# adaLN as dot products on VectorE over transposed weights, with its weight tiles dealt out anew

## The chip, the cores and the metric

The kernel runs on one core of a Trainium2 chip. The core has five engines with instruction streams of their own, which wait for each other by semaphores: TensorE (PE; its weight loads are PEld), VectorE (DVE), ScalarE (ACT), GpSimd (POOL) and SyncE (SP), here the issuer of most DMAs. The metric is the device time of one execution in microseconds.

## What is computed

Two transformer blocks over 256 tokens of 1024 channels in fp32, batch 1. The first block has two layers, each an adaLN, a hybrid mixer (gated linear attention and SSD), and a dense SwiGLU FFN (layer 0) or eight SwiGLU experts, top 2 (layer 1). The second block has one layer: adaLN, Hyena and neighbourhood attention, and PEER, which gathers rows of a table of 16384 experts. What the change touches is adaLN alone: three projections of a silu'd condition vector to 6 x 1024 values each, the third for two conditions.

```python
s = jax.nn.silu(c)
mod = s @ ada_w[l] + ada_b[l]                              # (1, 1024) @ (1024, 6144), l = 0, 1
sh1, sc1, g1, sh2, sc2, g2 = split(mod, 6)
h = rmsnorm(x, norm1_w[l]) * (1.0 + sc1) + sh1
x = x + g1 * hybrid_mixer(h, ...)
h = rmsnorm(x, norm2_w[l]) * (1.0 + sc2) + sh2
x = x + g2 * (swiglu(h, ...) if l == 0 else moe_swiglu(h, ...))
...
m = jax.nn.silu(cond) @ p['w_ada'] + p['b_ada']            # second block, for c and for c_ctx
```

## The kernel before

Activations lie transposed, channels on partitions (`xT`, `hT`: 128 x 8 x 256). Weights stream through `Ring`, five slots of 128 x 4096 fp32 (2 MB each). `place` hands the slots out in a fixed round, and SP, in `sp`, waits ahead of each load until the last user of that slot is done; so the loads are in a strict order, and one that waits holds all behind it. The experts' weights go through the same memory in halves (`parts`), and in PEER some of it holds gathered rows.

Each of the three adaLN matrices is 12 tiles of 512 output columns (class `Ada`, line 251), 2 MB each, 36 in all. The modulation has to end up with channels on partitions (`mods`), eight columns for each of the six vectors. For a tile and one condition, `ada_rows` (line 1192) on VectorE multiplies the eight 128 x 512 blocks of the tile by the eight columns of the condition and sums them into `accb`: one start (line 1199) and seven operations (line 1202). Then `ada_columns` (line 563) on TensorE sums `accb` over the partitions by four products with a column of ones, and `ada_add` (line 1206) on VectorE adds the bias and writes `mods`. `accb` is single: the rows of a tile wait until TensorE has read those of the one before (`acc_readers`). The tiles `ada2[0:4]` have two conditions and do all of it twice.

Four tiles (`ada0[0:4]`: shift and scale of the first norm) are done at the start. The others are dealt out by the list `behind` (line 262): six in mixer 0, twenty in the dense FFN, six in mixer 1 (`ada2[0:6]`, four of them with two conditions). They are worked off by `background()`, which stands at matching places of the streams of TensorE and VectorE; each call finishes the tile before and starts the next. In the mixers it stands behind the projections of z, qk, v and xs on TensorE and three times behind g, ahead of the state products (line 661); on VectorE behind `la`, behind the copies of q and k (lines 1250 and 1252), twice behind the copies of v (line 1274), and three times behind the scan `cum`, ahead of the states and the copy `dc` (line 1318). Lines 1256 to 1272 are the softplus, the scan and the exponentials of the gated linear attention, line 1284 its masked copies. In the FFN (line 747; lines 536 and 765 are the products) it stands three times in each of the seven steps; a step is gate and up (four pairs of 128 columns) and then the down product of the step before. SP loads in a step gate, up, two adaLN tiles, the down tile of the step before, and one more adaLN tile.

The second block's stage has no adaLN work. Its attention loop runs over 16 turns (8 heads x 2 halves of tokens): `peak(i + 2)` and `scaled(i + 1)` on VectorE, and between them TensorE's scores and transposes and ScalarE's copies and exponentials. TensorE works off eight pieces of gate projections (`fill`) beside q, k, kc and the first five turns. The bias of the attention holds one ring slot to the end of the loop.

PEER's dot products (line 1765) are `tensor_tensor_reduce` of 128 x 1024 from a gathered row tile and a token tile in PSUM, with a sum to one column; the trace calls them `CUSTOM_DVE_ANT_0`.

## Time and profile before

| | us |
|---|---|
| median of 3 runs | 3107.36 (3101.91 to 3108.8) |
| the profiled execution | 3108.38 |
| its span | 3106.6 |
| TensorE busy | 2660.6 (86%) |
| VectorE busy | 2012.0 (65%) |
| ScalarE busy | 1121.1 (36%) |

A row of a timeline gives start, duration, engine, line of the kernel, operation, output <- inputs and how many such instructions it merges; the brackets give the time that the engine was idle ahead of it, and what released it. Matmuls of fp32 appear as two instructions each. "ring" is a weight slot, "arena" the shared scratch, "ps" PSUM. Stages on the span: start to 47 us, mixer 0 to 255, dense FFN 272 to 619, mixer 1 642 to 872, experts 921 to 1925, second block to 2400, PEER to the end.

### The profile page before, as it was taken

The page shows a single profiled execution, that of the slowest core. Times are in us where ns is not written, and L with a number is a line of the kernel's source. Part 1 is how long each engine was busy: PE and PEld are TensorE (multiplying, and loading weights), DVE is VectorE, ACT ScalarE, POOL GpSimd, SP SyncE. Part 2 cuts the span into 40 slices and gives each one's busy share as a digit, 9 for nine tenths or more (in the row PEclk, how much of TensorE's full clock was granted, in tenths as well). Part 3 has the DMA queues.
Part 4 walks back from the last instruction along what each step waited for, and adds up shares of the span by engine and source line. Part 5 has one row for each costly group of instructions (what it writes and reads, how often), then busy time and mean ns, then how long its engine had stood idle before and what let it go on. Part 6 is the DMA issues. An engine that isn't in the chain of part 4 may idle for free. (4 is left out here: it accounts for less than half of the span.)

```text
span 3106.6 us, 34837 instructions
## 1 busy us (share of the span) xinstructions
PE 2660.6 (86%) x13674; PEld 2258.2 (73%) x13674; DVE 2012.0 (65%) x2882; ACT 1121.1 (36%) x1243; POOL 256.3 (8%) x280
## 2 busy tenths in 40 slices
PE   5866999986569999999999998699778898888787
PEld 4645788855457888888888886565666788887777
DVE  4553443346538889899998996353632777777764
ACT  1211000011127777777777775210340222222221
POOL 0000000000000000000000000000000233433341
PEclk8968999987669999999999999899898999988898
DMA  7702665635029999999999994521014799999996
GB/s 295 273 25 92 260 277 213 285 133 216 1 74 353 338 359 359 356 341 357 357 358 341 356 359 159 208 82 54 28 55 149 305 380 418 418 418 419 418 418 285
DMA packets 102139, 822.66 MB, mean 265 GB/s; under 512 B 11144, under 2 KB 13320, under 8 KB 13712
## 3 DMA queue, kind: packets, MB, share of 16 engines
q1 hardware_dynamic: 64816, 550.99, 46.3%
q0 software_dynamic: 36864, 268.45, 21.1%
q8 instruction: 111, 1.82, 0.2%
q10 hardware_dynamic: 288, 0.91, 0.1%
q14 instruction: 60, 0.49, 0.0%
HBM read 819.26 MB, written 1.05 MB: 264 GB/s over the span
## 5 line engine op out<-in xcount | busy, mean ns | idle before, releaser
L1491 DVE TENSOR_TENSOR ring_r<-ring,arena_r 128x2048 fp32r<-128x2048 f32 x336 | 770.2, 2292 | 12.2 <-ACT arena_r L1784 0.8
L1784 ACT ACTIVATE arena_r<-ring 128x2048 fp32r<-128x2048 f32 x336 | 645.0, 1920 | 10.7
L536 PE MATMUL ps<-h,ring 128*128 128x256 f32 (+1 forms) x2112 | 486.2, 393 | 48.8 <-ACT h L1784 31.8
L536 PEld LDWEIGHTS ps<-h,ring 128*128 128x128 f32 (+1 forms) x2112 | 408.0, 194 | 123.3 <-issue 53.6
L820 PE MATMUL ps<-arena_r 128*128 128x512 f32 x896 | 354.2, 395 | 1.5 <-DVE arena_r L1496 1.5
L822 PE MATMUL ps<-arena_r 128*128 128x512 f32 x896 | 349.7, 390 | 0.0
L821 PE MATMUL ps<-ring_r,arena_r 128*128 128x512 f32 x896 | 349.1, 390 | 0.0
L1784 ACT ACTIVATE arena<-ps 128x512 f32<-128x512 f32 (+2 forms) x204 | 103.2, 506 | 625.9 <-PE ps L536 415.7
L1144 PE MATMUL ps<-sel,arena 128*128 128x128 f32 x1904 | 254.4, 300 | 72.8 <-ACT sel L1784 72.8
L1144 PEld LDWEIGHTS ps<-sel,arena 128*128 128x128 f32 x1904 | 247.7, 215 | 79.4 <-ACT sel L1784 79.3
L1144 PE MATMUL ps<-sel,ring 128*128 128x128 f32 x2192 | 268.6, 285 | 41.1 <-ACT sel L1784 41.0
L1144 PEld LDWEIGHTS ps<-sel,ring 128*128 128x128 f32 x2192 | 262.2, 201 | 46.2 <-ACT sel L1784 46.0
L1202 DVE SCALAR_TENSOR_TENSOR accb<-ring,small,accb 128x512 f32<-128x512 f32 x280 | 210.5, 752 | 9.9
L1784 ACT ACTIVATE arena<-arena 128x4 f32<-128x4 f32 (+10 forms) x188 | 83.7, 445 | 360.2 <-DVE arena L1765 202.4
L1765 DVE CUSTOM_DVE_ANT_0 accb<-ring,ps 128x1024 f32<-128x1024 f32 x137 | 167.3, 1221 | 66.1 <-DMA ring<-in_uv,arena 63.1
L820 PEld LDWEIGHTS ps<-arena_r 128*128 128x128 f32 x896 | 168.3, 188 | 35.5 <-DVE arena_r L1496 1.8
L822 PEld LDWEIGHTS ps<-arena_r 128*128 128x128 f32 x896 | 168.3, 188 | 35.6
L821 PEld LDWEIGHTS ps<-ring_r,arena_r 128*128 128x128 f32 x896 | 168.5, 188 | 34.2
L1784 ACT ACT_TABLE_LOAD x62 | 79.5, 1283 | 301.6 <-DVE arena L1765 69.7
L1765 DVE CUSTOM_DVE_ANT_0 accb<-arena,ps 128x1024 f32<-128x1024 f32 x119 | 145.3, 1221 | 65.6 <-DMA arena<-in_uv,arena 63.3
L820 PE MATMUL ps<-arena_r,h_r 128*128 128x512 f32 x448 | 179.2, 400 | 6.6 <-DVE ring_r L1491 6.6
L822 PE MATMUL ps<-arena_r,h_r 128*128 128x512 f32 x448 | 175.9, 393 | 0.0
(237 smaller groups left out, 3037.6 us busy)
## 6 DMA issues: line engine op xcount, KB each, us to landing
ring<-in_moe_w_gate SPq DMA_DIRECT2D x112, 1024.0 KB, 5.8
ring<-in_moe_w_up SPq DMA_DIRECT2D x112, 1024.0 KB, 6.1
ring<-in_moe_w_down SPq DMA_DIRECT2D x112, 1024.0 KB, 5.6
ring<-in_ada_w SPq DMA_DIRECT2D x24, 2048.0 KB, 12.5
ring<-in_w_ada SPq DMA_DIRECT2D x12, 2048.0 KB, 10.4
ring<-in_w_in SPq DMA_DIRECT2D x10, 2048.0 KB, 11.3
ring<-in_ffn_w_gate SPq DMA_DIRECT2D x7, 2048.0 KB, 12.0
ring<-in_ffn_w_up SPq DMA_DIRECT2D x7, 2048.0 KB, 16.5
```

The lines of the kernel that those rows point to most:

```text
L536: last = e.matmul(out, a, b, start=(i == 0), stop=(i == len(pairs) - 1))
L820: e.matmul(out, xs[0], ws[0], start=start, stop=False, skip_group_check=True)
L821: e.matmul(out, xs[0], ws[1], start=False, stop=False, skip_group_check=True)
L822: return e.matmul(out, xs[1], ws[0], start=False, stop=stop, skip_group_check=True)
L1144: last = e.matmul(ps.banks[2 * t + c // 4][:, 128 * (c % 4):128 * (c % 4) + 128], rows[:, 1024 + 128 * c:1152 + 128 * c], m.diag[g % 2][:, ...
L1202: v(e.scalar_tensor_tensor(a, tile[:, k, :], t.s[:, i:i + 1], a, ALU.mult, ALU.add), ("rows", t.name))
L1491: v(e.tensor_tensor(m.low[parts.slot[unit]], parts.buf[unit], m.high[unit_at[unit] % NHIGH].bitcast(F32), ALU.subtract), ("low", unit))
L1765: v(e.tensor_tensor_reduce(m.waste, row_buffer(i)[0][:, 0:1024], x, 1.0, 0.0, ALU.mult, ALU.add, m.dots[:, i:i + 1]), ("dots", g))
L1784: A.mark(e.activation(out, src, func, **kw), name)
```

## The change

- The adaLN matrices are transposed on the host (`turned`): a tile of 2 MB holds 4 x 128 output channels on partitions, each with its 1024 weights in a row. The condition comes from the host repeated over the partitions (`cond`, 128 x 1024 each) and is silu'd on ScalarE there.
- A tile and condition is four `tensor_tensor_reduce` on VectorE (generator `ada`), each with the bias as the start value and one column of `mods` as the result. `ada_columns`, `ada_add` and `acc_readers` go. The product's elementwise output is dumped in `waste`.
- `some(pieces, n)` does n of these pieces at the places where `background()` stood on VectorE: 8, 4, 6 and 6 in a mixer; in the FFN 2 behind each activation, 3 in steps 2 to 5; 2 in each turn of the attention loop.
- The tiles are dealt out anew: four at the start and six in mixer 0 as before; fourteen in the FFN, two in each step, among them the four with two conditions; four in mixer 1 (16 pieces); eight in the attention loop.
- Loads: the FFN's step has five loads instead of six. In the second block the eight tiles are loaded behind `w_in`'s last tiles through the four slots other than that of the bias.
- The condition of the first block is loaded on ScalarE's queue between `pv` and `cs`; those of the second are loaded ahead of the norm behind mixer 0, and one of them again, into `accb`, ahead of the norm behind mixer 1.

```diff
-            def __init__(self, name, w, n, s, stride, ncond, bias, outs):
-                self.name, self.w, self.n, self.s, self.stride = (name, n), w[n], n, s, stride
-                self.ncond, self.bias, self.outs = ncond, bias, outs
-                self.at = n % 2 if name == "ada0" and n < 4 else 0
-        ada0 = [Ada("ada0", T["ada_w0"], n, small[:, 0:8], 1, 1, "ada_b0", [mod[0]]) for n in range(12)]
-        ada1 = [Ada("ada1", T["ada_w1"], n, small[:, 0:8], 1, 1, "ada_b1", [mod[1]]) for n in range(12)]
-        ada2 = [Ada("ada2", T["w_ada"], n, small[:, 8:24], 2, 2 if n < 4 else 1, "b_ada", [m2[:, 0, :], m2[:, 1, :]])
-                for n in range(12)]
-        behind = {"mix0": ada0[4:10], "ffn0": ada0[10:12] + ada1 + ada2[6:12], "mix1": ada2[0:6]}
+            def __init__(self, name, w, n, s, ready, bias, outs, waste):
+                self.name, self.w, self.n, self.s, self.ready = (name, n), w[n], n, s, ready
+                self.bias, self.outs, self.waste = bias, outs, waste
+        waste = arena[:, ARENA - 1024:ARENA]
+        cond0, cond1, cond2 = accb, arena[:, 2560:3584], arena[:, 3584:4608]
+        ada0 = [Ada("ada0", T["ada_w0"], n, [cond0], "silu c", "ada_b0", [mod[0]], waste) for n in range(12)]
+        ada1 = [Ada("ada1", T["ada_w1"], n, [cond0], "silu c", "ada_b1", [mod[1]], waste) for n in range(12)]
+        ada2 = [Ada("ada2", T["w_ada"], n, [cond1, cond2], "silu c2", "b_ada", [m2[:, 0, :], m2[:, 1, :]], waste)
+                for n in range(4)]
+        ada2 += [Ada("ada2", T["w_ada"], n, [accb], "silu c2 again", "b_ada", [m2[:, 0, :]], selb)
+                 for n in range(4, 12)]
+        behind = {"mix0": ada0[4:10], "ffn0": ada0[10:12] + ada1[0:2], "mix1": ada1[8:12], "second": ada2[4:12]}
+        for n in range(4):
+            behind["ffn0"] += [ada1[2 + n], ada2[n]]
+        behind["ffn0"] += ada1[6:8]
...
                         load(("up", f), T["ffn_w_up"][f])
-                        load_ada(hidden.pop(0))
-                        load_ada(hidden.pop(0))
+                        load_ada(hidden[2 * f])
+                        load_ada(hidden[2 * f + 1])
                         if f:
                             load(("down", f - 1), T["ffn_w_down"][f - 1])
-                        if hidden:
-                            load_ada(hidden.pop(0))
                     load(("down", 6), T["ffn_w_down"][6])
...
             load("bias", T["bias"])
+            kept = ring.slot["bias"]
+            ring.order, ring.n = [(kept + 1 + i) % NSLOT for i in range(NSLOT - 1)], 0
+            hidden = list(behind["second"])
             for n in range(8, 10):
                 load(("w_in2", 512 * n), T["w_in2"][n])
+                load_ada(hidden.pop(0))
+            for t in hidden:
+                load_ada(t)
             for name in ("w_hy", "w_na"):
                 for n in range(2):
                     load((name, n), T[name][n])
+            at = ring.n % (NSLOT - 1)
+            ring.order, ring.n = ring.order[at:] + ring.order[:at] + [kept], 0
             for n in range(2):
...
-            def ada_columns(t, among=range(8)):
-                b = bank(t.name, among)
-                e.wait_ge(*V["rows", t.name])
-                for c in range(t.ncond):
-                    for m in range(4):
-                        at = 512 * (t.at + c) + 128 * m
-                        last = e.matmul(b[:, 4 * c + m:4 * c + m + 1], accb[:, at:at + 128], ones[:, 0:1],
-                                        start=True, stop=True)
-                P.mark(last, t.name)
...
                 done(("w_in", l, "xs"))
-                background()
...
                 done(("w_in", l, "g"))
-                for _ in range(3):
-                    background()
...
-            def ada_rows(t):
-                tile = cols_of(t.name)
+            def ada(t):
+                tile = v4(ring.buf[t.name], 4)
                 e.wait_ge(*ring.loaded[t.name])
-                if acc_readers:
-                    e.wait_ge(*P[acc_readers.pop()])
-                for c in range(t.ncond):
-                    a = accb[:, 512 * (t.at + c):512 * (t.at + c) + 512]
-                    v(e.tensor_scalar(a, tile[:, 0, :], t.s[:, c:c + 1], None, ALU.mult))
-                    for k in range(1, 8):
-                        i = t.stride * k + c
-                        v(e.scalar_tensor_tensor(a, tile[:, k, :], t.s[:, i:i + 1], a, ALU.mult, ALU.add),
-                          ("rows", t.name))
-                ring.emptied[t.name] = V.now
-            def ada_add(t):
-                b = taken(t.name)
-                for c in range(t.ncond):
-                    v(e.tensor_tensor(t.outs[c][:, 4 * t.n:4 * t.n + 4], b[:, 4 * c:4 * c + 4],
-                                      pvc(t.bias, 4 * t.n, 4), ALU.add))
-                emptied(t.name)
+                e.wait_ge(*A[t.ready])
+                for m in range(4):
+                    o = 4 * t.n + m
+                    for s, out in zip(t.s, t.outs):
+                        v(e.tensor_tensor_reduce(t.waste, tile[:, m, :], s, 1.0, pvc(t.bias, o), ALU.mult, ALU.add,
+                                                 out[:, o:o + 1]))
+                        ring.emptied[t.name] = V.now
+                        yield
+            def some(pieces, n):
+                for _ in range(n):
+                    next(pieces, None)
             V.stage("ada")
             e.wait_ge(*in_pv)
-            e.wait_ge(*A["silu c"])
-            ada_rows(ada0[0])
+            some(ada(ada0[0]), 4)
             rstd(("norm1", 0), taken(("norm1", 0))[:, 0:256], 1.0 / D, scr_end[:, 2048:2304])
-            ada_rows(ada0[1])
-            for n in range(2):
-                ada_add(ada0[n])
-                ada_rows(ada0[n + 2])
-            for n in range(2, 4):
-                ada_add(ada0[n])
-            acc_readers.append(ada0[3].name)
+            for t in ada0[1:4]:
+                some(ada(t), 4)
...
-                background()
+                some(hidden, 8)
                 v(e.tensor_scalar(m.qT, v4(taken(("qk", l, 0)), 2), 0.125, None, ALU.mult))
                 emptied(("qk", l, 0))
                 v(e.tensor_copy(m.kT, v4(taken(("qk", l, 1)), 2)))
                 emptied(("qk", l, 1))
-                background()
+                some(hidden, 4)
...
-                for _ in range(2):
-                    background()
+                some(hidden, 6)
...
-                for _ in range(3):
-                    background()
+                some(hidden, 6)
...
-                        if j == 1:
-                            background()
-                    background()
-                    background()
+                        some(hidden, 3 if 2 <= f < 6 else 2)
...
+            hidden = chain.from_iterable(ada(t) for t in behind["second"])
             for i in range(16):
                 if i + 2 < 16:
                     peak(i + 2)
                 if i + 1 < 16:
                     scaled(i + 1)
+                some(hidden, 2)
             ring.emptied["bias"] = V.now
...
+            e.dma_start(cond0, T["cond"][0]).then_inc(in_c[0], 16)
             e.dma_start(cs, T["cs"]).then_inc(in_cs[0], 16)
             A.stage("ada")
             e.wait_ge(*in_pv)
-            a(small[:, 0:8], pvc("c", 0, 8), ACT.Silu, "silu c")
-            a(small[:, 8:24], pvc("c2", 0, 16), ACT.Silu, "silu c2")
+            e.wait_ge(*in_c)
+            a(cond0, cond0, ACT.Silu, "silu c")
...
+                e.wait_ge(*in_c2)
+                for cond in (cond1, cond2):
+                    a(cond, cond, ACT.Silu, "silu c2")
...
+                e.wait_ge(*in_c2_again)
+                a(accb, accb, ACT.Silu, "silu c2 again")
...
+                if l == 0:
+                    for cond, src in ((cond1, T["cond"][1]), (cond2, T["cond"][2])):
+                        e.dma_start(cond, src).then_inc(in_c2[0], 16)
+                else:
+                    e.dma_start(accb, T["cond"][1]).then_inc(in_c2_again[0], 16)
                 norm(("norm2", l), xT, mod[l][:, 24:32], hT, scr_end, ("hT", "norm2", l))
...
+    def turned(w):
+        return w.T.reshape(-1, 4, 128, 1024).transpose(0, 2, 1, 3).reshape(-1, 128, 4096)
...
+        "cond": np.repeat(np.stack([x["c"][0], x["c_2"][0], x["c_ctx_2"]])[:, None, :], 128, axis=1),
```

## Rows read from the trace of the kernel before

**Rows 1.** Stages: start:end, length, PE, PEld, DVE, ACT, POOL busy, PEclk, DMA share, GB/s.

```profile
272.20:619.40 347.20, 323.55 (x1504) 284.74 (x1504) 130.01 (x208) 12.01 (x29) 0.00 (x0) 0.94 0.58 239
...
921.00:1925.00 1004.00, 997.50 (x4613) 830.30 (x4614) 894.80 (x554) 727.79 (x478) 0.00 (x0) 1.00 0.91 341
```

**Rows 2.** Groups by line on VectorE: shapes, count, busy us, mean ns, idle before.

```profile
L1202 DVE SCALAR_TENSOR_TENSOR accb<-ring,small,accb 128x512 f32<-128x512 f32 x280 | 210.5, 752 | 9.9
...
L1765 DVE CUSTOM_DVE_ANT_0 accb<-ring,ps 128x1024 f32<-128x1024 f32 x137 | 167.3, 1221 | 66.1 <-DMA ring<-in_uv,arena 63.1
```

**Rows 3.** Timeline of VectorE in PEER: start us, us, engine, line, operation.

```profile
2453.72 1.22 DVE L1765 CUSTOM_DVE_ANT_0 accb<-ring,ps 128x1024 f32<-128x1024 f32 x1
...
2454.99 1.22 DVE L1765 CUSTOM_DVE_ANT_0 accb<-ring,ps 128x1024 f32<-128x1024 f32 x1
```

**Rows 4.** Timeline of the start, all engines; in brackets idle time before and its releaser.

```profile
1.17 0.47 ACTq L1809 DMA_DIRECT2D cs<-in_cs  x1
...
13.28 5.59 PE L536 MATMUL ps<-arena,cs 128*128 128x256 f32 x16 [13.28 <-DMA cs<-in_cs]
...
19.24 0.42 DVE L1170 TENSOR_SCALAR arena<-ps 128x256 f32<-128x256 f32 x1
...
21.49 0.49 DVE L1199 TENSOR_SCALAR accb<-ring,small 128x512 f32<-128x512 f32 x1
...
41.98 0.16 DVE L1209 TENSOR_TENSOR mods<-ps,pv 128x4 f32<-128x4 f32 x1 [1.83 <-PE ps L570]
```

**Rows 5.** Timeline of VectorE in mixer 0.

```profile
92.23 0.69 DVE L1252 COPY arena<-ps 128x512 f32<-128x512 f32 x1 [6.21 <-PE ps L536]
...
99.25 0.43 DVE L1256 TENSOR_SCALAR arena<-arena 128x512 f32<-128x512 f32 x1
...
113.72 1.42 DVE L1274 COPY arena<-ps 128x512 f32<-128x512 f32 x2
...
128.87 2.67 DVE L1284 COPY_PREDICATED arena<-ms,ps 128x128 f32<-128x128 uint32 x8
...
139.77 0.49 DVE L1199 TENSOR_SCALAR accb<-ring,small 128x512 f32<-128x512 f32 x1
...
162.82 0.19 DVE L1318 COPY arena<-ps 128x32 f32<-128x32 f32 x1
```

**Rows 6.** Timeline of TensorE in mixer 0.

```profile
106.59 0.95 PE L570 MATMUL ps<-cs,accb 128*128 128x1 f32 x8
...
124.70 13.98 PE L536 MATMUL ps<-h,ring 128*128 128x256 f32 x64
...
155.90 5.08 PE L661 MATMUL ps<-arena 128*128 128x256 f32 x12
```

**Rows 7.** Timeline of VectorE in mixer 1.

```profile
686.35 0.69 DVE L1252 COPY arena<-ps 128x512 f32<-128x512 f32 x1 [6.21 <-PE ps L536]
...
700.49 0.43 DVE L1256 TENSOR_SCALAR arena<-arena 128x512 f32<-128x512 f32 x1
...
745.10 2.67 DVE L1284 COPY_PREDICATED arena<-ms,ps 128x128 f32<-128x128 uint32 x8
...
777.85 0.19 DVE L1318 COPY arena<-ps 128x32 f32<-128x32 f32 x1
```

**Rows 8.** Timeline of TensorE in the dense FFN.

```profile
272.22 29.98 PE L536 MATMUL ps<-h,ring 128*128 128x256 f32 x128 [8.68 <-ACT h L1784]
...
315.74 16.59 PE L536 MATMUL ps<-h,ring 128*128 128x256 f32 x64 [4.34 <-issue]
...
347.68 14.06 PE L765 MATMUL ps<-arena,ring 128*128 128x256 f32 x64
```

**Rows 9.** Loads into the ring, 290 to 380 us (dense FFN): issue to landing.

```profile
DMA to landing us min/median/max: 7.5/13.3/17.7
```

**Rows 10.** Timeline of VectorE in the attention loop.

```profile
2276.79 0.42 DVE L1653 SCALAR_TENSOR_TENSOR arena<-ps,ring 128x256 f32<-128x256 f32 x1 [7.03 <-ACT arena L1784]
...
2281.12 0.42 DVE L1653 SCALAR_TENSOR_TENSOR arena<-ps,ring 128x256 f32<-128x256 f32 x1 [1.99 <-ACT arena L1784]
```

60 lines of the change are left out of this document (8 added, 52 removed).

## The prediction, made before the change was run

> **What bounds the kernel now.** I read the view by stages first. In the experts' stage TensorE is busy 997.5 of 1004 us at a granted clock of 1.00 (2.4 GHz), so nothing that VectorE does is worth anything there, and the change leaves that stage alone. In the dense FFN it is busy 323.55 of 347.20 us: 24 us are open [rows 1]. The time lies where TensorE and VectorE wait for each other, so I read both engines' timelines through the two mixers, the FFN and the attention loop. In mixer 0 the projections of g end at 138.7, but the state products start only at 155.9 [rows 6]: between them stand the tiles of adaLN, one after the other, VectorE's rows, TensorE's columns, VectorE's addition. Their operands are ready; the queue order holds them back. In mixer 1, with two conditions in four of its six tiles, the same piece of code runs from 686.35 to 777.85, 91.5 us, against 70.6 us (92.23 to 162.82) in mixer 0 [rows 5, 7].
>
> **Price of a piece.** Before, a tile costs seven operations of 752 ns [rows 2] and a start, some 6 us, then columns and an addition. After, it is four dot products of 128x1024, each one `tensor_tensor_reduce`. The same operation stands in PEER: 1221 ns, and one starts 1.27 us after the other, 2453.72 to 2454.99 [rows 2, 3]. I take 1.27 us. That row reads one operand from PSUM, the new ones both from SBUF, so the price is not quite shown: a lower one has no row for it; the upper end is a rival, below. The rows operation at 752 ns for 512 columns has two SBUF operands and against 1221 ns for 1024 it shows no doubling [rows 2].
>
> The Trainium skill speaks against this ("Vector Engine (DVE) Microarchitecture Reference", "Points that are easy to get wrong"): a scalar_tensor_tensor with two non-bf16 SBUF sources halves throughput, as both read ports are taken and none is left for the accumulator's readback. By it a piece would be some 2.2 to 2.3 us by estimate, and the sum would be that of the second rival. The rows operation in this trace, two fp32 sources in SBUF without an accumulator, isn't slowed; with one, no row shows it.
>
> **The parts, by stage** (times on the axis of before).
> 1. Start. Old: the last addition ends at 41.98 + 0.16 [rows 4]. New: four tiles are 16 pieces, 20.3 us, and the 2.25 us of the norm's root (19.24 to 21.49 [rows 4]) in front of the last twelve. The condition, now 512 KB, goes on ScalarE's queue ahead of `cs`. `cs` was issued at 1.17 and held the first TensorE work until 13.28 [rows 4]: with `pv` some 890 KB in 12.5 us, 71 KB a us, so half a MB more delays the norm by up to 7.4 us, and at the 341 GB/s of the experts' stage [rows 1] by 1.5. VectorE's root starts then at 20.7 to 26.6 instead of 19.24 [rows 4], and 2.25 + 12 x 1.27 later it is done: 38.1 to 44.0. That is a gain of 4 to a loss of 2; I take the middle, a gain of 1.
> 2. Mixer 0. Copy of k done at 92.9, four pieces 5.1: the softplus starts at 98.0 instead of 99.25; its chain to the end of the copies of v, 15.9 us, ends at 113.9; six pieces: 121.5 [rows 5]. TensorE loses three column groups ahead of the end of g (0.95 us each [rows 6], counted at 0.8 since they overlap their neighbours), which comes at 136.3 instead of 138.7 [rows 6]. VectorE's masked copies to the scan took 10.9 us (128.87 to 139.77) [rows 5], 1.6 of it the addition and its wait (as the 1.83 at 41.98 [rows 4]): 9.3, so 130.8; six pieces: 138.4. From the start of the state products to the copy behind them are 6.9 us (155.90 to 162.82) [rows 5, 6]: 136.3 + 6.9 = 143.2; VectorE alone would be there at 143.0. Gain 162.8 - 143.2 = 19.6. What is late next is TensorE's own projections; the tiles are there, since their slots come free with z, qk and v as before.
> 3. FFN. By 7 steps: gate and up 28.1 us, down 14.06 [rows 8]. Before, six tiles a step went through five slots; now five, so each kind has its slot. Gate and up of the next step are issued together when the products of this one end, land within 13.3 us [rows 9], and the down products of 14.06 us [rows 8] cover that by 0.4 (without this cover it costs the difference in each of five steps). Step 1 has no down in front; its gate already has a free slot and only up must land, 7.5 [rows 9] + 0.4, taken as 8. Sum: 29.98 + 8 + (16.59 + 14.06) + 5 x 28.1 + 7 x 14.06 = 307.6, against 347.2 [rows 1, 8]: gain 39.6. VectorE has 12 pieces, 15 us, in steps of 42 us; two activations of the broadcast conditions and their loads lie beside the norm and the first products.
> 4. Mixer 1, by the same steps: copy of k done at 687.0 [rows 7], +5.1, +15.9, four last pieces +5.1: 713.1; masked copies and scan: 725. g ends 43.4 us behind the copy of k (136.3 - 92.9): 730.4; +6.9 = 737.3, instead of 777.85 [rows 7]. Gain 40.5. VectorE has 5 us of slack there.
> 5. ScalarE issues two loads ahead of the norm behind mixer 0, one behind mixer 1, 0.47 us each [rows 4], on the chain: loss 1.4. The activation in `route` lies beside the router's products.
> 6. Attention. Eight tiles, two pieces in each of 16 turns. In the first five, TensorE's gate projections fill the turn: VectorE waits 7.03 us [rows 10], hidden. In the nine behind them a turn takes 4.33 us (2276.79 to 2281.12) of which VectorE waits 1.99 and works 2.34 [rows 10]; 2.54 doesn't fit: 2.34 + 2.54 + 0.04 = 4.92, loss 9 x 0.59 = 5.3. Bounds 0 and 9 x 2.54 = 23, if the pieces stood wholly on the chain; they stand just where it waits for ScalarE, so 5.3. SP's queue: w_in's last tiles wait for slots between adaLN's, w_hy and w_na behind them; by the order of slots each is issued some 10 us or more before it is read.
>
> Sum: 1 + 19.6 + 39.6 + 40.5 - 1.4 - 5.3 = 94.0. The profiled execution took 3108.4; the median of the runs is 1.0 below it. 3107.4 - 94.0 = 3013.4, rounded to 3014.
>
> **Rivals.**
> - Loads stay the bound of the FFN. The longest landing there is 17.7 us [rows 9], with three tiles in line. If gate and up take that, each of five steps waits 4 us, and its first half goes at the pace of 16.59 instead of 14.06 [rows 8]: 5 x 6.5 = 33 lost, 3046; without the slower half 3034. For it: cover and landing are 0.4 us apart. Against: 17.7 had a third tile ahead.
> - Two SBUF operands halve the dot product. From rows, (1221 - 752) / 512 x 1024 = 0.94 us more [rows 2], some 2.3 with doubts. Start -11, mixer 0 +3 (16 exposed pieces), mixer 1 +40.5 (its slack takes it), FFN +39.6 (29 of 42 us), loads -1.4, attention 9 x 2.7 = -24: 46 gained, 3062. The skill's sentence above would be this case.
> - Slower than before: the price of a piece on VectorE where it is exposed: twelve at the start, sixteen and eight in the mixers, eighteen in attention, 54 in all. From 2.3 us the remaining 46 us are gone after another 0.85: it decides from about 3.2 us a piece. At 4 us the FFN's 12 pieces a step (50 us) also exceed 42: some 3180. Against it: 1221 ns [rows 2] shows nothing near it.
> - The change doesn't do what it says: the column products would still be there. The calls are gone from the code, so this is left at nothing.
>
> **How the numbers follow.** Forecast 0.70; FFN loads 0.13; halved dot 0.11; slower 0.03; the gains in the mixers given back by something that I don't see, with no change within 0.2%, 0.03. Each unknown in the first case: start +3 or -3, attention +5 or -18 at its ends, FFN 0 to -20. Low end 3014 - 3 - 5 = 3006, taken as 3003; high end 3042, which takes in most of the loads' case. 0.2% (6 us) is about what a measurement of this kernel can tell from no change: faster 0.94, same 0.02, slower 0.04.
>
> **What would show it.** Custom operations in the adaLN lines near 1.22 us (2.2: second rival). State products of mixer 0 right behind g, and 70.6 and 91.5 us of that code both near 50. FFN near 308 us with five steps of 42.2; idle TensorE in front of each gate product would show the first rival. Turns of 4.9 us in the second half of attention. Experts' stage and PEER as long as before; if either moved by more than 3 us, the sum is wrong in a place that I hadn't looked at.

## The result, and the profile after

| | before | after |
|---|---|---|
| median, us | 3107.12 (3101.91 to 3108.8) | 3002.5 (2996.93 to 3007.13) |
| span of the profiled execution, us | 3106.6 | 3003.0 |
| TensorE busy, us | 2660.6 | 2596.3 |
| VectorE busy, us | 2012.0 | 1983.8 |

The ratio is 0.9665, with a 95% interval of 0.9644 to 0.9687: 104.6 us less by the medians, 103.6 by the spans. The forecast was 94.0 less, 3014 us, with a range of 3003 to 3042: the median lies half a microsecond below its low end, and the four runs on both sides of it. VectorE works only 28 us less than before. TensorE works 64 us less and is idle for 406.7 us of the span instead of 446.0, so of the gain some 64 us are TensorE's own busy time and 39 its waits.

Since only spans of stages can be compared with the steps of the forecast, here is where the 103.6 us lie. Each number is the time from one event of the timelines to the next. Of the forecast's 1.4 us for loads on ScalarE's queue, 0.9 belong ahead of the FFN and 0.5 behind mixer 1.

| stage, from and to | before | after | gain | forecast |
|---|---|---|---|---|
| start, to TensorE's first projection | 47.40 | 48.77 | -1.4 | +1 |
| mixer 0, to the copy of the decay (`dc`) | 115.42 | 97.41 | +18.0 | +19.6 |
| to the FFN's first product | 109.40 | 109.70 | -0.3 | -0.9 |
| FFN, on TensorE | 347.15 | 303.33 | +43.8 | +39.6 |
| end of FFN to mixer 1's copy of the decay | 158.48 | 114.81 | +43.7 | +40.5 |
| rest of mixer 1 and experts, to the final norm | 1157.84 | 1152.35 | +5.5 | -0.5 |
| final norm to attention's first masked copy | 287.53 | 294.25 | -6.7 | 0 |
| attention, first to last masked copy | 88.66 | 94.33 | -5.7 | -5.3 |
| to the first MAX8 of PEER | 99.26 | 97.10 | +2.2 | 0 |
| PEER | 695.46 | 690.95 | +4.5 | 0 |

Timeline of VectorE of the kernel after in mixer 0: the copy of k, then from the scan to the copy that answers to the last row of [rows 5]. One piece is a dot product and the read of its accumulator, and the next starts 1.33 us later. The state products on TensorE were started at 137.91, right behind the products of g (next fence); the copies of the state wait for the sixth piece, not for them.

```profile
94.59 0.69 DVE L1205 COPY arena<-ps 128x512 f32<-128x512 f32 x1 [6.21 <-PE ps L550]
...
133.13 0.68 DVE L1251 TENSOR_TENSOR_SCAN arena<-cs,arena 8x256 f32<-8x256 f32 x1
133.85 1.28 DVE L1170 CUSTOM_DVE_ANT_0 arena<-ring,accb,pv 128x1024 f32<-128x1024 f32 x1
135.06 0.08 DVE L1170 DVE_READ_ACCUMULATOR2_ANT mods<- 128x1 f32 x1
135.18 1.28 DVE L1170 CUSTOM_DVE_ANT_0 arena<-ring,accb,pv 128x1024 f32<-128x1024 f32 x1
...
141.82 1.26 DVE L1264 COPY arena<-ps 64x128 f32<-64x128 f32 x4
...
146.18 0.19 DVE L1269 COPY arena<-ps 128x32 f32<-128x32 f32 x1
```

TensorE in the same place, to be held against [rows 6], with the state products of mixer 1 as its last row, and behind it VectorE in mixer 1, against [rows 7]: there VectorE has four pieces behind the copies of v and none behind the scan, and waits 6.71 us for the state products.

```profile
124.09 13.98 PE L550 MATMUL ps<-h,ring 128*128 128x256 f32 x64
137.91 2.77 PE L647 MATMUL ps<-arena 128*128 128x256 f32 x12
...
668.52 2.76 PE L647 MATMUL ps<-arena 128*128 128x256 f32 x12
```

```profile
625.21 0.69 DVE L1205 COPY arena<-ps 128x512 f32<-128x512 f32 x1 [6.21 <-PE ps L550]
...
669.66 1.26 DVE L1264 COPY arena<-ps 64x128 f32<-64x128 f32 x4 [6.71 <-PE ps L647]
...
674.02 0.19 DVE L1269 COPY arena<-ps 128x32 f32<-128x32 f32 x1
```

TensorE in the FFN, to be held against [rows 8]. The products of gate and up of all later steps take 27.8 us in one piece, the down products 13.98, and the only wait of more than 0.3 us that is left is that ahead of step 1, 8.11 us.

```profile
255.88 29.60 PE L550 MATMUL ps<-h,ring 128*128 128x256 f32 x128 [8.49 <-ACT h L1722]
293.59 29.52 PE L550 MATMUL ps<-h,ring 128*128 128x256 f32 x128 [8.11 <-issue]
322.94 13.98 PE L743 MATMUL ps<-arena,ring 128*128 128x256 f32 x64
337.19 27.86 PE L550 MATMUL ps<-h,ring 128*128 128x256 f32 x128 [0.28 <-issue]
364.90 13.98 PE L743 MATMUL ps<-arena,ring 128*128 128x256 f32 x64
```

VectorE in one later turn of the attention loop, against [rows 10]. From one start of L1589 to the next are 5.04 us, and no bracket is left: the wait of 1.99 us is filled by two pieces of 1.33, and the turn is VectorE's.

```profile
2179.23 0.42 DVE L1589 SCALAR_TENSOR_TENSOR arena<-ps,ring 128x256 f32<-128x256 f32 x1
...
2181.09 0.48 DVE L1599 TENSOR_SCALAR arena<-arena 128x512 f32<-128x512 f32 x1
2181.61 1.28 DVE L1170 CUSTOM_DVE_ANT_0 sel<-ring,accb,pv 128x1024 f32<-128x1024 f32 x1
...
2182.93 1.28 DVE L1170 CUSTOM_DVE_ANT_0 sel<-ring,accb,pv 128x1024 f32<-128x1024 f32 x1
...
2184.26 0.42 DVE L1589 SCALAR_TENSOR_TENSOR arena<-ps,ring 128x256 f32<-128x256 f32 x1
```

Three questions follow. Does a piece cost what the forecast says it costs, and where? How much of the gain is the arithmetic, how much the dealing of the tiles, and how much the order in the queues? And to whom belong the last rows of the table, of which the forecast says nothing?

### The profile page after: what moved, and what is told of

Its sections match the earlier page's. It is cut to its first block and busy times, and to the rows that moved or that the text cites. A ratio compares the mean times of both kernels' runs of the same rounds, so it can differ in the third digit from the quotient of the medians.

```text
span 3003.0 us, 34097 instructions
## 1 busy us (share of the span) xinstructions
PE 2596.3 (86%) x13354; PEld 2193.5 (73%) x13354; DVE 1983.8 (66%) x2842; ACT 1127.1 (38%) x1246; POOL 257.6 (9%) x280
## 5 line engine op out<-in xcount | busy, mean ns | idle before, releaser
L550 PE MATMUL ps<-h,ring 128*128 128x256 f32 (+1 forms) x2112 | 473.7, 386 | 58.3 <-ACT h L1722 49.6
L550 PEld LDWEIGHTS ps<-h,ring 128*128 128x128 f32 (+1 forms) x2112 | 400.1, 190 | 133.7 <-issue 75.0
L793 PE MATMUL ps<-ring_r,h_r 128*128 128x512 f32 x448 | 175.6, 392 | 0.0
```

The lines of the kernel that those rows point to most:

```text
L550: last = e.matmul(out, a, b, start=(i == 0), stop=(i == len(pairs) - 1))
L793: e.matmul(out, xs[0], ws[1], start=False, stop=False, skip_group_check=True)
```

## The experiments

### What a piece costs at each place

Every dot product is made twice, in the kernel after:

```diff
                     for s, out in zip(t.s, t.outs):
-                        v(e.tensor_tensor_reduce(t.waste, tile[:, m, :], s, 1.0, pvc(t.bias, o), ALU.mult, ALU.add,
-                                                 out[:, o:o + 1]))
+                        for _ in range(2):
+                            v(e.tensor_tensor_reduce(t.waste, tile[:, m, :], s, 1.0, pvc(t.bias, o), ALU.mult,
+                                                     ALU.add, out[:, o:o + 1]))
```

> The kernel after, with every dot product of adaLN made twice in a row (160 more, 1.33 us each, same result): what a piece costs at each place. My theory is that a piece counts only where VectorE has no wait left. Start: 12 pieces behind the root stand on the chain, 12 x 1.33 = 16, and the first four eat the 4.75 us wait, so 16.6 more. Mixer 0: the first eight hide in VectorE's 16.18 us wait for q, the other sixteen don't: 21.3 more. Mixer 1: eight hidden, the other eight cost 10.6 less the waits of 6.71 and 1.20 us: 3 more. FFN: 24 pieces, 32 us, in a step of 41.9: 0 to 2 more. Attention: the first five turns absorb them (3.2 to 4.37 us of wait are left), then 9 or 10 turns x 2.66: 24 to 27 more. Sum +66 to +70: about 3070 us. Rival: VectorE is busy in only 66% of the span of the kernel after, so most of the extra 213 us falls into waits everywhere, mixer 0 and attention included: under +20, below 3023. Second rival: every piece counts, +213.

Measured: 3072.56 us, 0.9883 of before (0.9866 to 0.9899); span 3070.6, 67.6 more than the kernel after. By stages, with the expectation in brackets: start 16.5 (16.6), mixer 0 21.2 (21.3), FFN 0.0 (0 to 2), mixer 1 from the copy of k on 2.8 (3), attention 21.2 (24 to 27). The stretch ahead of the FFN was 2.3 us longer and that behind the attention loop 2.6, of which nothing had been expected; the first of them varies by as much between two profiles of the same kernel (last section of the experiments). One later turn of attention, VectorE: from one L1590 to the next 7.69 us, 2.65 more than above for two pieces more, and again without a bracket.

```profile
2225.58 0.42 DVE L1590 SCALAR_TENSOR_TENSOR arena<-ps,ring 128x256 f32<-128x256 f32 x1
...
2227.96 1.28 DVE L1171 CUSTOM_DVE_ANT_0 sel<-ring,accb,pv 128x1024 f32<-128x1024 f32 x1
...
2233.27 0.42 DVE L1590 SCALAR_TENSOR_TENSOR arena<-ps,ring 128x256 f32<-128x256 f32 x1
```

Both rivals are out. VectorE's share of 66% says nothing of where a piece is free: 160 pieces, 213 us, cost 67.6. They are free in the FFN and in the first eight of each mixer, and cost in full at the start behind the root, in mixer 0 behind the copy of k, and in attention's later turns. There it was eight turns, not nine or ten. The other eight pieces of mixer 1, which the forecast counts among its 54 exposed ones, cost 2.8 us of 10.6. So the forecast's list of places holds but for these eight and for attention's count, 16 pieces instead of 18; its price does not quite, 1.33 us and not 1.27. A piece that costs 2.66 us is also close to what the rival of the halved dot product meant: half the rate of the 1.22 us of [rows 3] would be some 2.5 us a piece, where the forecast took 2.3, so its time would have come out a little below 3070 and not at 3062.

### Arithmetic or dealing

The kernel after with as many tiles in each stage as before (6, 20, 6, none):

```diff
...
-        behind = {"mix0": ada0[4:10], "ffn0": ada0[10:12] + ada1[0:2], "mix1": ada1[8:12], "second": ada2[4:12]}
-        for n in range(4):
-            behind["ffn0"] += [ada1[2 + n], ada2[n]]
-        behind["ffn0"] += ada1[6:8]
...
+        behind = {"mix0": ada0[4:10], "ffn0": ada0[10:12] + ada1 + ada2[0:6], "mix1": ada2[6:12], "second": []}
...
                         if f:
                             load(("down", f - 1), T["ffn_w_down"][f - 1])
+                        if hidden:
+                            load_ada(hidden.pop(0))
```

With it went that the pieces of the FFN are four behind each activation from step 1 on, and that the condition of the second block is loaded into `accb` one stage earlier, ahead of mixer 1.

> The kernel after, with as many tiles in each stage as before the change (6 in mixer 0, 20 in the FFN, 6 in mixer 1, none in attention), which tiles they are being chosen so that each has its condition at hand: the arithmetic alone, without the new dealing. My theory: in the FFN six loads a step go through five slots again, and TensorE's idle time there goes back from 8.4 us towards the 23.65 us of before: +15 (8 to 20). Mixer 1 gets eight more pieces, the copies of the state become VectorE's: +3. Attention has turns of 4.33 us instead of 5.04: -7. Sum +11: about 3014 us (3005 to 3022). Rival: loads don't bound the FFN and the new dealing was worth nothing: -7 or more, 2996 or below. Second rival: the dealing brought a large part of the whole gain: over +30, 3033 or more.

Measured: 3045.26 us, 0.9792 of before (0.9776 to 0.9809). The second rival is right, and my number for the FFN was far off: it takes 340.49 us, 37.2 more than in the kernel after, where I had 15. Mixer 1 is 2.8 longer from the copy of k on (3 expected), the attention loop 5.3 shorter (88.99 against 94.33). TensorE in the FFN:

```profile
298.40 30.54 PE L547 MATMUL ps<-h,ring 128*128 128x256 f32 x128 [12.80 <-issue]
328.77 13.98 PE L740 MATMUL ps<-arena,ring 128*128 128x256 f32 x64
348.47 29.41 PE L547 MATMUL ps<-h,ring 128*128 128x256 f32 x128 [5.72 <-issue]
377.71 13.98 PE L740 MATMUL ps<-arena,ring 128*128 128x256 f32 x64
396.11 29.48 PE L547 MATMUL ps<-h,ring 128*128 128x256 f32 x128 [4.42 <-issue]
```

SyncE's queue shows why. In each step the sixth load is taken up first, ahead of gate and up, when TensorE ends its products:

```profile
377.91 0.33 SPq L443 DMA_DIRECT2D ring<-in_ada_w  x1
378.28 0.43 SPq L443 DMA_DIRECT2D ring<-in_ffn_w_gate  x1
378.75 0.43 SPq L443 DMA_DIRECT2D ring<-in_ffn_w_up  x1
```

And the view of the transfers, between 250 and 560 us, has the tile of up landing 17.4 us behind its issue in this kernel (first line, a median) and 12.9 in the kernel after (second line). The down products that cover it take 13.98. Whether six loads would fit if the sixth stood behind gate and up wasn't tried, so the number of loads and the place of this one aren't told apart.

```profile
ring<-in_ffn_w_up SPq DMA_DIRECT2D x6, 2048.0 KB, 17.4
```

```profile
ring<-in_ffn_w_up SPq DMA_DIRECT2D x6, 2048.0 KB, 12.9
```

What I had wrong: I took the 23.65 us in which TensorE stood idle in the FFN before [rows 1] for the whole price of the loads. But the column products of 20 tiles, 19.87 us of TensorE's busy time, stood largely inside the waits for loads. Take them away and TensorE's busy time falls from 323.55 to 304.05 us, but its idle time rises to 36.5 of 340.5 us:

```profile
256.10:596.60 340.50, 304.05 (x1344) 263.50 (x1344) 135.94 (x220) 13.63 (x31) 0.00 (x0) 0.94 0.59 244
```

### The same question from the other side

The kernel before, its arithmetic untouched, with 14 tiles in the seven steps of the FFN and five loads a step, and the other six behind it:

```diff
                         if f:
                             load(("down", f - 1), T["ffn_w_down"][f - 1])
-                        if hidden:
-                            load_ada(hidden.pop(0))
                     load(("down", 6), T["ffn_w_down"][6])
+                    for t in hidden:
+                        load_ada(t)
...
                     if f:
                         down(f - 1)
-                    background()
                 down(6)
-                if due:
-                    ada_columns(due.pop())
+                while hidden or due:
+                    background()
```

VectorE's stream has the same change.

> The kernel before, with its old arithmetic, where only 14 tiles of adaLN are loaded and worked in the seven steps of the FFN, five loads a step; the other six follow behind the last down products, one after the other, which costs some 50 us by itself, so only the FFN up to its last down product is to be read. My theory, from old_counts (new arithmetic with six loads a step: 340.4 us, against 303.3 with five and 347.2 before): the loads set the pace, the column products lie in their waits, and with five loads the old arithmetic takes 303 + 14 x 1.2 of columns = 320 us, 27 less than before. Rival: the old arithmetic is bound by itself (rows, columns, addition in turn and the slow first half of each gate product at 16.6 instead of 14.06), and the stage stays at 340 or more. Whole time: 3107 - 27 + 50 = 3130.

Measured: 3119.51 us, 1.0044 of before (1.0030 to 1.0058), and the FFN up to its last down product 312.64 us instead of 347.15. The rival is out, and even my 320 was too much. The six tiles behind the FFN cost what it gained: from its end to mixer 1's copy of the decay are 205.58 us instead of 158.48. The column products of the other tiles now stand in the open, 0.95 us each and about 0.8 on the chain, and no wait is left in these steps:

```profile
354.28 13.98 PE L536 MATMUL ps<-h,ring 128*128 128x256 f32 x64
368.09 0.95 PE L570 MATMUL ps<-cs,accb 128*128 128x1 f32 x8
368.90 14.06 PE L536 MATMUL ps<-h,ring 128*128 128x256 f32 x64
382.80 0.95 PE L570 MATMUL ps<-cs,accb 128*128 128x1 f32 x8
383.61 14.06 PE L765 MATMUL ps<-arena,ring 128*128 128x256 f32 x64
```

With the two kernels of above this is a square for the FFN:

| FFN, us | six loads a step | five loads a step |
|---|---|---|
| old arithmetic | 347.15 | 312.64 |
| new arithmetic | 340.49 | 303.33 |

Fewer loads are worth 34.5 to 37.2 us, the new arithmetic 6.7 to 9.3. The 34.5 hold some 5 us of column products, since six tiles left the stage with their loads. All this is time of the FFN alone: six tiles are worked elsewhere, and the new arithmetic is what makes them cheap there, as in attention, where eight tiles cost 5.3 us. Whether the old arithmetic, dealt out the same way with tiles in the attention loop, would keep much of the gain wasn't tried; it is a rival that stays open.

### Order or work

The kernel before, with the last three steps of adaLN in each mixer behind the state and decay work, on both queues:

```diff
                 done(("w_in", l, "g"))
-                for _ in range(3):
-                    background()
...
                             P.mark(last, ("o", l, h))
+                for _ in range(3):
+                    background()
```

```diff
                   ("cum", l))
-                for _ in range(3):
-                    background()
...
                                           m.dc[:, 0, 8 + h:9 + h], ALU.subtract), ("cb", l, p))
+                for _ in range(3):
+                    background()
                 e.wait_ge(*A["xin", l])
```

> The kernel before, with its old arithmetic, in which the last three steps of adaLN in each mixer stand behind the state and decay work instead of ahead of it, on TensorE's and VectorE's queue alike: the order alone. My theory is that the work had to go, not only its place: the state products of mixer 0 start right behind g, near 137 instead of 155.9, but the rows of three tiles, some 6 us each, then stand ahead of the convolution on VectorE, which sets the pace there, and the gain is given back within the mixer: the whole time within 8 us of before, 3100 to 3110. Rival: the order of the queues was the cause, and most of the 17 us in mixer 0 and up to half of the 43 us in mixer 1 come without any new arithmetic: 3070 or below.

Measured: 3106.8 us, 0.9997 of before (0.9988 to 1.0007). The state products of mixer 0 start at 138.27, right behind g and at the full clock (2.77 us instead of 5.08), and the copy of the decay comes at 143.77 instead of 162.82 [rows 5], in mixer 1 too 19.1 us sooner behind the copy of k (72.42 instead of 91.50). But by the first product of the FFN 12 of the 19 us are given back. TensorE's state products, and VectorE:

```profile
138.27 2.77 PE L659 MATMUL ps<-arena 128*128 128x256 f32 x12
```

```profile
140.70 3.03 DVE L1313 SCALAR_TENSOR_TENSOR arena<-arena,ps 64x128 f32<-64x128 f32 x8
154.23 5.48 DVE L1202 SCALAR_TENSOR_TENSOR accb<-ring,small,accb 128x512 f32<-128x512 f32 x7
162.51 5.47 DVE L1202 SCALAR_TENSOR_TENSOR accb<-ring,small,accb 128x512 f32<-128x512 f32 x7
170.73 1.53 DVE L1335 SCALAR_TENSOR_TENSOR arena<-arena,pv 128x256 f32<-128x256 f32 x3
```

An x7 at L1202 is one tile. The rows of the tiles now stand in front of the convolution. The order of the queues made the wait visible at the state products, but with the old work the order alone gives nothing that can be measured in the whole time. The gain isn't all lost in the mixers, though: in the profiled execution this kernel was still 13.1 us ahead of the kernel before at the sums of the final norm (1922.57 against 1935.69). Behind them it lost 5.6 us up to the attention loop and 2.9 us in it, 2.6 of these in the third turn, though the edit touches neither. The first of the two stretches is taken up below; the second stays open.

### Attention's pieces, moved to where VectorE waits

The forecast's step 6 says that the first five turns have room and the later ones don't. So:

```diff
-                some(hidden, 2)
+                some(hidden, (4, 3, 4, 5, 5)[i] if i < 5 else 1)
```

> The kernel after, with the 32 pieces in attention dealt as 4, 3, 4, 5, 5 to the first five turns, where VectorE still waits 3.2 to 4.4 us a turn, and one to each later turn, which has 1.99 us free without pieces. My theory: the later turns go back from 5.04 us to 4.33, 9 or 10 x 0.7 = 6 to 7 less, and nothing is lost in the first five: about 2997 us. Rival: the tiles aren't there so early (they are issued some 8 us apart from 2133 on), VectorE waits for them in the first turns, and the gain is lost or turned round: 3003 or more. Second rival: a later turn isn't bound by VectorE but by ScalarE and TensorE at 5.04: no change.

Measured: 3014.3 us, 0.9704 of before (0.9688 to 0.9720): some 12 us more than the kernel after. The loop takes 107.38 us instead of 94.33. VectorE, three of its pieces:

```profile
2131.68 1.28 DVE L1170 CUSTOM_DVE_ANT_0 sel<-ring,accb,pv 128x1024 f32<-128x1024 f32 x1 [2.57 <-DMA ring<-in_w_ada]
...
2151.01 1.28 DVE L1170 CUSTOM_DVE_ANT_0 sel<-ring,accb,pv 128x1024 f32<-128x1024 f32 x1 [11.19 <-issue]
...
2175.57 1.28 DVE L1170 CUSTOM_DVE_ANT_0 sel<-ring,accb,pv 128x1024 f32<-128x1024 f32 x1 [9.20 <-DMA ring<-in_w_ada]
```

The first rival, and the reason is in the ring: with four slots in turn, the third and the fifth tile stand behind the two last tiles of w_in, whose products are made in these very turns. Later turns were at 4.33 us again, with a few at 4.46 to 4.78, so the second rival is out. Hence a second try, with the slots dealt by hand:

```diff
-            ring.order, ring.n = [(kept + 1 + i) % NSLOT for i in range(NSLOT - 1)], 0
+            four = [(kept + 1 + i) % NSLOT for i in range(NSLOT - 1)]
+            ring.order, ring.n = [four[i] for i in (0, 1, 2, 3, 1, 3, 0, 1, 3, 0, 2, 1, 3, 0)], 0
...
-            at = ring.n % (NSLOT - 1)
-            ring.order, ring.n = ring.order[at:] + ring.order[:at] + [kept], 0
+            ring.order, ring.n = [four[i] for i in (2, 1, 3, 0)] + [kept], 0
...
-                some(hidden, 2)
+                some(hidden, (4, 3, 4, 4, 5)[i] if i < 5 else 1 + (i == 15))
```

> As front_turns, which lost some 12 us in the attention loop since VectorE waited 2.57, 11.19 and 9.20 us for tiles that stood behind the slots of the last two tiles of w_in. Here the tiles of adaLN go through the other slots in turn, and none waits for those two until their products are made; 4, 3, 4, 4, 5 pieces in the first five turns, one in each later turn, two in the last. My theory: the placement was right and only the slots were wrong: the loop from the first masked copy to the last takes 94.33 us in the kernel after and 88.99 without any pieces, and here about 89 to 90: 4 to 5.5 less, about 2998 us. Rival: with two slots in rotation a tile lands each 8 to 10 us, one short of what the turns of 9.4 us want, and VectorE still waits: the loop at 94 or more.

Measured: 2996.55 us, 0.9641 of before (0.9624 to 0.9658), the loop 89.40 us: 4.9 less than in the kernel after, and 0.4 more than with no pieces at all (88.99, old_counts). One wait for a tile is left, 2.49 us in the second turn, and behind it VectorE still waits 0.59 us for ScalarE, so it costs nothing.

### The start

```diff
             some(ada(ada0[0]), 4)
+            some(ada(ada0[1]), 4)
             rstd(("norm1", 0), taken(("norm1", 0))[:, 0:256], 1.0 / D, scr_end[:, 2048:2304])
-            for t in ada0[1:4]:
+            for t in ada0[2:4]:
```

> The kernel after, with the second tile's four dot products of the start moved ahead of the root of the norm, into VectorE's wait of 4.75 us. Nothing else. My theory: the second tile has landed by 20.6 us, the start is bound by VectorE's 16 dot products and the root, and the first projection starts at about 44.4 instead of 48.77: 4.4 less, about 2998 us. Rival: the tiles of the start come no faster than VectorE takes them now (8 MB behind 1 MB of x), and the wait only moves: 0 to 1 us.

Measured: 2996.19 us, 0.9634 of before (0.9617 to 0.9651); the first projection starts at 43.87 instead of 48.77. All 16 pieces and the root follow one another without a wait from 15.14 on:

```profile
24.45 1.28 DVE L1170 CUSTOM_DVE_ANT_0 arena<-ring,accb,pv 128x1024 f32<-128x1024 f32 x1
...
25.77 0.42 DVE L1142 TENSOR_SCALAR arena<-ps 128x256 f32<-128x256 f32 x1
...
28.02 1.28 DVE L1170 CUSTOM_DVE_ANT_0 arena<-ring,accb,pv 128x1024 f32<-128x1024 f32 x1
```

So the start is VectorE's, and not that of its loads; the second tile was there.

### The wait of step 1 in the FFN

```diff
                     hidden = list(behind["ffn0"])
+                    load(("gate", 0), T["ffn_w_gate"][0])
+                    load(("up", 0), T["ffn_w_up"][0])
+                    load_ada(hidden[0])
                     for f in range(7):
-                        load(("gate", f), T["ffn_w_gate"][f])
-                        load(("up", f), T["ffn_w_up"][f])
-                        load_ada(hidden[2 * f])
-                        load_ada(hidden[2 * f + 1])
                         if f:
+                            load_ada(hidden[2 * f - 1])
                             load(("down", f - 1), T["ffn_w_down"][f - 1])
+                            load_ada(hidden[2 * f])
+                        if f < 6:
+                            load(("gate", f + 1), T["ffn_w_gate"][f + 1])
+                            load(("up", f + 1), T["ffn_w_up"][f + 1])
                     load(("down", 6), T["ffn_w_down"][6])
+                    load_ada(hidden[13])
```

The pieces on VectorE are dealt to match, with four behind the last step.

> The kernel after, with the loads of the FFN in another order: gate and up of step 1 are loaded in step 0, the second adaLN tile of step 0 behind them, and so in every step; five loads a step as now, one tile's dot products behind the last step. My theory: TensorE's only wait in the FFN, 8.11 us ahead of step 1, goes away, since it was a free slot that up lacked, and the FFN takes 295.2 instead of 303.3 us: about 2995 us. The 14 us of down products still cover gate and up of the later steps. Rival: an adaLN tile now stands behind up and ahead of down in every step, its landing falls into the time of the others, and some 2 to 4 us a step of waiting come in place of the 8: no gain, up to 10 us slower.

Measured: 2989.9 us, 0.9614 of before (0.9598 to 0.9630); the FFN takes 292.79 us. TensorE's first two products of gate and up are one row now:

```profile
255.34 57.20 PE L555 MATMUL ps<-h,ring 128*128 128x256 f32 x256 [8.51 <-ACT h L1728]
312.38 13.98 PE L748 MATMUL ps<-arena,ring 128*128 128x256 f32 x64
326.65 18.58 PE L555 MATMUL ps<-h,ring 128*128 128x256 f32 x85 [0.30 <-issue]
```

It gains 10.5 where the wait was 8.11. Most of the rest is the clock: behind the wait the products of step 1 took 29.52 us in the kernel after, with a granted clock of 0.77 from 293.6 to 301.0 us and of 1.00 from there on; those behind the wait at the stage's start took 29.60 (0.78 in their first 8 us), against 27.8 in the steps without one. Here both steps together take 57.20, and from 284 to 312 us the granted clock is 1.00. TensorE is busy for 292.46 of 292.80 us: the FFN has nothing left but its products.

### All three

The edits of the last three kernels together (start, FFN, slots and turns of attention).

> The kernel after with the three edits that each gained by themselves: the root of the norm behind eight dot products at the start (the first projection came 4.90 us earlier), gate and up of step 1 loaded in step 0 (the FFN took 292.79 instead of 303.33 us), and attention's pieces in the first five turns with slots in turn (its loop took 89.40 instead of 94.33 us). My theory: they lie in three stages one behind the other and add up, 4.9 + 10.5 + 4.9 = 20.3 less than the kernel after: 2982 us, 0.960 of before. Rival: part of it is taken back where the stages meet or by TensorE's clock: 2990 or more.

Measured: 2981.03 us, 0.9591 of before (0.9576 to 0.9606); 21.5 us less than the kernel after by the medians, 20.3 expected. They add up. This version is faster than both kernels.

### What repeats and what doesn't

The kernel after, once more:

> The kernel after, unchanged: how far stages of the same instructions differ between two profiled executions. My theory: the stages before the tail of mixer 1 repeat within 0.5 us, while the stretches in which TensorE works in short bursts (tail of mixer 1, the norms behind the experts) differ by 3 to 10 us with the clock that is granted there, and so the 5.3 us that mixer 1's tail gained and the 6 us that were lost behind the experts are not the change's. PEER repeats within 1 us near 691, 2.5 to 4.8 us shorter than in the three profiles of kernels of the old arithmetic. Rival: tail and norms repeat too, and both differences belong to the change.

Measured: 3003.22 us (3000.57 to 3005.28), span 3001.0. The FFN (303.45), both mixers from the copy of k on (51.59 and 48.81), the attention loop (94.32) and PEER (690.70) repeat within 0.3 us. The tail of mixer 1, from the copy of the decay to the sums of the next norm, took 93.05 us in the first profile and 89.56 in this one. In the view by stages VectorE's and ScalarE's busy times are the same and TensorE's clock isn't (0.72 and 0.77 of 2.4 GHz on the mean, so parts of it at 1.2 GHz); the stretch in the first profile, then in the second:

```profile
674.00:767.00 93.00, 55.12 (x255) 44.72 (x255) 49.21 (x93) 16.93 (x23) 0.00 (x0) 0.72 0.10 37
```

```profile
675.50:765.10 89.60, 50.81 (x255) 41.17 (x256) 49.22 (x94) 16.91 (x23) 0.00 (x0) 0.77 0.11 39
```

The same stretch of the kernel before was 96.95 us in one profile and 95.5 in another (old_cond_array, below, the same instructions), with clocks of 0.70 and 0.73. Between the pair of profiles of the table it gained 3.9 us, and between the better ones of each kernel 5.9. Which execution was profiled moves it by 1.5 to 3.5 us, but all eight profiles with the edited kernel's 16 pieces in mixer 1 took 89.6 to 93.1 us and the three with the old arithmetic in its old place 95.5 to 97.0: this gain goes with the change, and the forecast doesn't have it. The new arithmetic alone doesn't bring it: old_counts, with 24 pieces in mixer 1, took 95.8. It is at least in part the clock: in the kernel before, the 64 products of 128x256 at its line 722 took 15.92 us and in the kernel after (line 708) 13.97. Why TensorE is granted more there isn't shown.

The stretch behind the experts, where the forecast's table has -6.7, did repeat here (294.30), against my expectation. But it stands at two levels, whatever the kernel: 287.53 and 287.75 in two profiles of old arithmetic and 293.12 and 293.13 in two others; 293.8 to 294.5 in nine of the new, and 287.15 in one, front_turns, whose instructions up to there are those of the kernel after. The sums of the final norm in the kernel after, and in front_turns:

```profile
1826.37 7.16 PE L550 MATMUL ps<-arena,cs 128*128 128x256 f32 x16 [8.29 <-ACT arena L1722]
```

```profile
1823.56 5.12 PE L550 MATMUL ps<-arena,cs 128*128 128x256 f32 x16 [8.58 <-ACT arena L1722]
```

Sixteen equal products, 7.16 and 5.12 us, each behind 8 us of idle time, at a granted clock of 0.54 and 0.72. So the 6.7 us can't be put down to the change; that the long level comes more often with the new arithmetic, in nine profiles of ten against two of four, is too few to tell.

PEER took 690.7 to 691.7 us in every profile of the new arithmetic and 693.5 to 695.5 in those of the old. Two kernels asked whether the place of its table in memory does it, which the new input array shifts:

```diff
+        "cond": np.repeat(np.stack([x["c"][0], x["c_2"][0], x["c_ctx_2"]])[:, None, :], 128, axis=1),
         "uv": np.concatenate([x["peer_u_2"][0], x["peer_v_2"][0]], axis=1), "bias": bias,
```

> The kernel before with one more input array in the chip's memory, that of the broadcast conditions (1.5 MB), declared where the kernel after has it and read by nobody. From the first MAX8 of PEER to the end, kernels of the old family took 693.5 to 695.5 us and those of the new 690.7 to 691.7, and their gathers moved 418 and 420 to 421 GB/s in the middle. Theory: the place of the gathered table in memory makes that difference, and this kernel takes 691 and shows 420 to 421. Rival: it is something else (slots, what stands in front of PEER): 694 and 418 again.

and in the kernel after, the same line moved behind all the others:

> The kernel after with the array of the broadcast conditions declared last, so that the gathered table stands in memory where it would without it. Theory of the place in memory: from the first MAX8 to the end 693.5 to 695.5 us, and 418 GB/s in the middle, as in the kernel before. Rival: 691 and 420 to 421, as in the kernel after: the place has nothing to do with it.

Measured: 693.80 us with the array in the old kernel, 690.97 with the array last in the new (whole times 3107.86 and 3001.37). The array's place has nothing to do with it. The gathers' rate does differ, 418 GB/s in all old profiles and 420 to 421 in all new ones, in the middle of PEER; why is left open. The ring comes into PEER in another order of slots; front_turns_slots and all_three change that order once more and take 691.4 and 691.2 us at the same rate, so not every change of it shows, and more wasn't tried.

## Why the prediction was right, and where it was off

The time, 3002.5 us, is 11.5 below the forecast of 3014 and 0.5 below the low end of its range. The mechanisms were those that were forecast; what came out larger are the FFN and mixer 1, for which the range had only a loss or nothing, and stages that the sum leaves out. That the sum came within 10 us is partly luck: it holds misses of +7.4 (FFN and mixer 1), +5.5 (mixer 1's tail and experts) and +4.5 (PEER) against -4.0 (start and mixer 0) and -6.7 (the stretch ahead of attention).

**Price of a piece.** 1.28 us and 1.33 from start to start, where I took 1.27 from the dot product in PEER [rows 2, 3], which reads PSUM for one operand and takes 1.22. With both operands in SBUF it takes 0.06 us more. The Trainium skill ("Vector Engine (DVE) Microarchitecture Reference", "Points that are easy to get wrong") has a scalar_tensor_tensor with two non-bf16 SBUF sources at half throughput, with no port left for the accumulator; this dot product, with two fp32 operands in SBUF and an accumulator, isn't halved in the trace: 1.28 us against 1.22 with one operand in PSUM. Whether it is the operation that the page means can't be told, since the trace records it as a custom one. The rival of the halved dot product falls either way; double_pieces shows what it would have done. Its 2.2 to 2.3 us a piece were too few for a halved rate: twice 1.22 is 2.44.

**Start.** +1 forecast, -1.4 came. The term that was off is the norm's root: I took the middle of its range, and it came at 25.35 us, near the late end (20.7 to 26.6), because `cs` stands behind the conditions in the queue: TensorE's sums, which wait for it, started at 19.25 us instead of 13.28. In its shadow VectorE waited 4.75 us, which root_later takes back.

**Mixer 0.** The step holds: state products right behind g, 137.91 (136.3 forecast). I had both engines at 143, and in fact it was VectorE that came last, with the copy of the decay at 146.18: its sixth piece ended at 141.82, where the state products, by the 1.14 us that VectorE's copies follow them in mixer 1 (668.52 to 669.66), would have let it go at 139.1. From the first projection to that copy are 97.41 us, 1.6 more than the forecast's 95.8. About 1.0 of it came ahead of the copy of k (45.82 us behind the first projection instead of 44.83; the stage's first products took 9.93 us instead of 8.95, at a granted clock of 0.71 instead of 0.78), and 1.0 is 0.06 for each of sixteen pieces. 51.59 us for the code that took 70.59, where I had expected near 50.

**FFN.** The mechanism was right and it was the loads, as the step says: the square above shows 34.5 to 37.2 us for five loads instead of six. The wait of step 1 was 8.11 us (8 forecast), and the cover of 14 us held (waits of 0.25 and 0.28 in two steps). The 4.2 us that I missed are in the size of the products: 27.8 us for gate and up where I took 28.1 from [rows 8] (some 2.1 us in five steps), 29.52 for step 1 where I took 16.59 + 14.06 (1.3), and the rest in the down products. A row's 14.06 us run 0.16 us into the next instruction (332.97 to 346.87 from start to start in the kernel before), which the sum counted each time; and the 16.59 of before stood behind a wait, with a granted clock of 0.69 in its first 8 us where the kernel after has 0.77. The rival in which loads stay the bound would have needed 17.7 us to land, and that is what old_counts shows with three tiles in line (17.4); with two it was 12.9.

**Mixer 1.** 40.5 forecast, 43.7 came. From the copy of k to that of the decay 48.81 us instead of 91.50, with 6.71 us of VectorE's slack (5 forecast; the forecast's own terms, 713.1 and 9.3, give 722.4 and not the 725 that it states, so some 8 us of slack; with the 1.20 us that VectorE waited for TensorE ahead of the masked copies it was 7.9). The term that was too large is the 6.9 us from the state products to the copy, taken from a row of mixer 0 in which the products ran at a granted clock of 0.55 (5.08 us for 12 of them, behind the columns and their waits); here they took 2.76 us at 1.00, and the 6.9 became 5.5. Another 0.7 is in the products ahead, and 1.0 came ahead of the copy of k. In mixer 0 the same speed was worth nothing, since VectorE came last.

**Loads on ScalarE's queue.** 0.9 us of the 1.4 were forecast ahead of the FFN, 0.3 measured in a stretch that varies by over 2 us between profiles of the same instructions (109.70 and 112.06). It can't be seen.

**Attention.** -5.3 forecast, -5.7 came, by two errors that cancel: eight full turns instead of nine, and 0.71 us each instead of 0.59. Behind it 2.2 us came back, 1.45 of them in the w_hy products (27.89 us instead of 29.34), behind a stretch at a granted clock of 0.68 instead of 0.50.

**What I said wouldn't move.** "Experts' stage and PEER as long as before; if either moved by more than 3 us, the sum is wrong in a place that I hadn't looked at." The experts' products didn't (1000.2 and 1000.1 us from the first to the end of the last). PEER did, by 4.5 in this pair of profiles and by some 3 over all, and this stays unexplained; the sum is wrong there, as the sentence says. Mixer 1's tail and the experts, of which the tail isn't named in the forecast, gave 5.5, of them 3.9 in the tail. So of the 9.6 us between 94.0 and 103.6, some 7 are mis-sized terms in FFN and mixer 1 less 4 in the start and mixer 0, and the rest is tail, final norm, PEER and small terms, of both signs, most of which no run explains.

## What to carry to other kernels

Waits for loads hide work, and when that work is taken away the wait takes its place: idle time in a stage isn't the price of its loads, and removing the hidden work alone gave 7 us of the FFN where one load fewer a step, worked elsewhere, gave 37. Ask of each idle stretch on a second engine how many microseconds fit in and by when its data have landed, and whose slot they wait for; moving pieces to where VectorE is free lost 12 us until the slots were moved with them. Count what a piece costs at its place, not by the engine's share: 160 pieces of 1.33 us on an engine that is busy for 66% cost 68 us.

## What the runs showed of the hardware

A dot product of 128x1024 fp32 with accumulator takes 1.28 us from two SBUF operands and 1.22 with one in PSUM. In the FFN two tiles of 2 MB issued together landed in 8.8 and 12.9 us, and behind a third the last took 17.4. Behind an idle stretch of 8 us TensorE's products there ran at a mean granted clock of 0.77 over the next 7.4 us (so partly at 1.2 and partly at 2.4 GHz) and at 1.00 from there on, which made 27.8 us of them 29.5. The clock in stretches of short bursts isn't the same from one execution to the next: sixteen equal products took 7.16 or 5.12 us, mixer 1's tail 93.05 or 89.56 and the stretch behind the experts 294 or 287. Runs of the kernel after spread over 10 us (2996.93 to 3007.13); that these stretches make up that spread is likely but not shown. A term below some 5 us is to be read from its stage, and a stage of short bursts from more than one profile.
